# One transformer block pair on one core: norms read from PSUM, Tanh for Sigmoid and Exp, the second residual moved to VectorE, and a last output block in one PSUM region

## The reference, cut to what matters

```python
y = conv_gated_mlp(rms_norm(h, ln_ffn_pre), w_up, conv_w, conv_b, w_down)
h = h + rms_norm(y, ln_ffn_post)
h = h + (p @ w_pe) * sigmoid(h @ w_pg)            # end of the first block
...                                               # second block: projections u @ w_in
conv, forgetting and memory heads: head output * silu(gate)
h = h + concat(heads) @ w_out
return rmsnorm(h, final_g)                        # final_g is a vector of 2048
```

## Time and profile before

| | us |
|---|---|
| median of 3 runs | 1853.12 (1852.43 to 1854.91) |
| profiled execution, its own time | 1853.38 |
| its span, first to last instruction | 1851.6 |
| TensorE busy in the span | 1800.9 |
| VectorE, ScalarE, GpSimd busy | 1282.6, 960.8, 653.2 |
| mean granted TensorE clock | 0.992 of full |

### The profile page before, as it was taken

One profiled execution on the slowest core, in us unless ns is written; L12 is line 12 of the kernel. 1 busy time (PEld: TensorE's weight loads), 2 busy tenths in 40 slices (PEclk: granted clock), 3 DMA queues, 4 the chain that ended last, 5 costly groups with the idle time before them and its releaser, 6 DMA issues.

```text
span 1851.6 us, 29943 instructions
## 1 busy us (share of the span) xinstructions
PE 1800.9 (97%) x10306; PEld 1569.7 (85%) x10306; DVE 1282.6 (69%) x1584; ACT 960.8 (52%) x1276; POOL 653.2 (35%) x639
## 2 busy tenths in 40 slices
PE   9999999999989999999999999999899999999996
PEld 7888888888878888888888888888788888878885
DVE  6676666665578777777777544446787778888754
ACT  5564555445456555555555433335555666764532
POOL 3723444444743333211111322223452255450033
PEclk9999999999999999999999999999899999999998
DMA  8434444445554555555555455555455444443452
GB/s 316 146 132 159 160 161 164 172 160 205 187 206 179 193 187 181 184 192 190 181 183 195 163 187 187 187 187 191 145 193 195 144 175 159 159 159 137 161 188 105
DMA packets 50284, 326.56 MB, mean 176 GB/s; under 512 B 5696, under 2 KB 6336, under 8 KB 17600
## 3 DMA queue, kind: packets, MB, share of 16 engines
q1 hardware_dynamic: 49664, 323.86, 49.4%
q10 hardware_dynamic: 576, 2.11, 0.3%
HBM read 323.85 MB, written 2.10 MB: 176 GB/s over the span
## 4 chain that ended last, share of the span: by engine, by line
PE 83%; DVE 7%; issue 4%; ACT 3%; DMA 1%; SPq 1%; POOL 0%; DVEq 0%; ACTq 0%; POOLq 0%
PE ps L1759 52%; PE ps L1760 27%; DVE wlo L926 2%; PE ps_lev L1834 2%; ACT whi L438 1%; DMA stage<-in_w_a 1%; DVE fge L949 1%; DVE fs L1477 1%; PE ps_t L1788 0%; ACT usq L814 0%; DVE fge L1481 0%; DVE tmp L932 0%; DVE y L1219 0%; ACT small L445 0%; PE ps_t L2065 0%
## 5 line engine op out<-in xcount | busy, mean ns | idle before, releaser
L1759 PE MATMUL ps<-act_a,whi 128*128 128x512 f32 x3072 | 1092.3, 397 | 10.7 <-DVE tmp L932 8.4
L926 DVE TENSOR_TENSOR wlo<-stage,whi 128x2048 fp32r<-128x2048 f32 (+1 forms) x316 | 701.5, 2221 | 248.8 <-ACT whi L438 244.9
L1760 PE MATMUL ps<-act_a,wlo 128*128 128x256 f32 x3072 | 869.3, 283 | 0.0
L1759 PEld LDWEIGHTS ps<-act_a,whi 128*128 128x128 f32 x3072 | 578.5, 188 | 144.9 <-DVE tmp L932 7.7
L438 ACT ACTIVATE whi<-stage 128x2048 fp32r<-128x2048 f32 (+1 forms) x316 | 568.9, 1801 | 122.4 <-DMA stage<-in_w_down 105.5
L1760 PEld LDWEIGHTS ps<-act_a,wlo 128*128 128x128 f32 x3072 | 579.0, 188 | 0.3
L1759 PE MATMUL ps<-big,whi 128*128 128x512 f32 x1600 | 566.0, 396 | 9.1 <-DVE big L1333 7.3
L1760 PE MATMUL ps<-big,wlo 128*128 128x256 f32 x1600 | 453.4, 283 | 0.0
L1759 PEld LDWEIGHTS ps<-big,whi 128*128 128x128 f32 x1600 | 301.5, 188 | 80.1 <-DVE big L1333 5.6
L445 ACT ACTIVATE small<-ps 128x256 f32<-128x256 f32 x248 | 94.8, 382 | 520.4 <-PE ps L1760 520.3
L1760 PEld LDWEIGHTS ps<-big,wlo 128*128 128x128 f32 x1600 | 301.9, 189 | 0.1
(11 more groups left out here) (338 smaller groups left out, 1400.9 us busy)
## 6 DMA issues: line engine op xcount, KB each, us to landing
stage<-in_w_a SPq DMA_DIRECT2D x166, 1024.0 KB, 4.8
stage<-in_w_b SPq DMA_DIRECT2D x87, 1024.0 KB, 4.8
stage<-in_w_down SPq DMA_DIRECT2D x64, 704.0 KB, 4.0
stage<-in_w_a SPq DMA_DIRECT2D x8, 256.0 KB, 9.7
mem_raw<-in_memT SPq DMA_DIRECT2D x1, 2048.0 KB, 9.2
mem_again<-in_memT SPq DMA_DIRECT2D x1, 2048.0 KB, 9.1
out<-o_out SPq DMA_DIRECT2D x4, 512.0 KB, 2.7
x_in<-in_xT ACTq DMA_DIRECT2D x3, 512.0 KB, 8.8
```

Source lines behind the costliest of these rows:

```text
L926: dve.tensor_tensor(wlo[:, slot, part], stage[:, slot, part], whi[:, slot, part].bitcast(F32), ALU.subtract).then_inc(w_lo, 1)
L1759: pe.matmul(dst, whi[:, slot, c * P:(c + 1) * P], act, start=start, stop=False)
L1760: return pe.matmul(dst[:, T:2 * T], wlo[:, slot, c * P:(c + 1) * P], act[:, 0:T], start=False, stop=stop)
```

## The change

It is one diff with these parts. They are numbered as the prediction takes them.

1. Norms: `mean_square` is gone for all norms but "uc". ACT's Ln reads the sum from PSUM with scale 1/2048 and a bias column `eps`. `ln_ahead()` loads the Ln table earlier (start, before `G_OUT`, after the first residual, last down block, before conv, before `G_OUT2`). POOL's squares of `h4` wait on "h3_norm".
2. Gates: Sigmoid and the Exp of the gates become Tanh. The gate is made with (tanh + 1) by one `scalar_tensor_tensor` on DVE, with factors 0.5 and 0.25 in neighbouring instructions. `logistic` (add one, reciprocal) is gone.
3. The "y" stage: the last tile of `y` is squared by ACT; all of the residual is on DVE, quarter after quarter; the 16 outputs of `w_pe` lie in pairs in seven banks and ACT copies two at once; the first two blocks of `w_pg` are run together, quarter by quarter.
4. `fox_turned` of the last head stands in the middle of the second memory block; `memory_turned` and `memory_out` of the last memory head move one block later.
5. The last block of `G_OUT2` goes to one region of 256 columns: identity by `h`'s last tile, then three matmuls of 256 columns for a cell. ACT squares it from PSUM. DVE alone scales the output, in five pieces; there are five output DMAs.

```diff
+        eps = sb("eps", [P, 1])
+        y_sq = over("y_sq", a_at, 23 * KB, [P, T])
+        out_parts = (slice(0, 4), slice(4, 8), slice(8, 12), slice(12, 14), slice(14, 16))
+        pair_banks = [*wide_banks, ps_sc[:, :], ps_t[:, :], bank_b[:, :], ps[:, 0, :], ps[:, 1, :]]
@@ sync
-            for c in range(QUARTERS):
-                sp.wait_ge(*(s("o_ready"), c + 1) if c < QUARTERS - 1 else (s("o_last"), 1))
-                sp.dma_start(out[:, quarter(c), :], o_out[:, quarter(c), :]).then_inc(s("out_done"), 16)
+            for n, part in enumerate(out_parts):
+                sp.wait_ge(s("o_ready"), n + 1)
+                sp.dma_start(out[:, part, :], o_out[:, part, :]).then_inc(s("out_done"), 16)
@@ scalar
-            def norm(t, name):
-                inverse_root(t, event(name + "_ms"), event(name + "_norm")[0])
+            def ln_ahead():
+                act.preload_act_table(ACT.Ln)
+
+            def norm(t, name, sums):
+                act.wait_ge(*event(name + "_summed"))
+                link(act.activation(t, sums, ACT.Ln, scale=1.0 / D, bias=eps[:, 0:1]))
+                act.activation(t, t, ACT.Exp, scale=-0.5).then_inc(event(name + "_norm")[0], 1)
@@
-            def sigmoid(e, x, lin, done, i):
+            def tanh(e, x, lin, done, i, scale=1.0):
                 wait(act, lin, i + 1)
-                act.activation(e[:, :], x[:, :], ACT.Sigmoid).then_inc(s(done), 1)
+                act.activation(e[:, :], x[:, :], ACT.Tanh, scale=scale).then_inc(s(done), 1)
@@ last down block
-                        act.activation(dummy[:, 1:2], ones[:, 0:1], ACT.Ln)
+                        ln_ahead()
+                        act.wait_ge(out_free, U_DOWN + KT + 2)
+                        act.wait_ge(*step("y_acc", KT - 1))
+                        act.activation(y_sq[:, :], y[:, KT - 1, :], ACT.Square).then_inc(step("y_acc", 0)[0], 1)
@@
-            keep(range(3))
-            norm(rstd[:, :], "y")
-            keep(range(3, 7))
+            norm(rstd[:, :], "y", ps_a)
             hi(G_PE, 0, 0, 3)
-            keep(range(7, 11))
+            keep(range(4))
             split_h2(0)
-            keep(range(11, 13))
+            keep(range(4, 7))
             split_h2(1)
-            keep(range(13, 16))
+            keep(range(7, 8))
             split_h2(2)
             split_h2(3)
@@
-            for j in range(4):
+            for j in range(3):
                 evac(U_OUT2 + 12 + j, j % 2, G_OUT2 - U_OUT2)
...
-            act.wait_ge(s("h4_ready"), KT)
-            act.activation(sq4[:, 1, :], h4[:, KT - 1, :], ACT.Square).then_inc(event("h4_last_sq")[0], 1)
-            norm(rstd[:, :], "h4")
+            act.wait_ge(w_used, N_BLOCKS)
+            act.activation(sq4[:, 1, :], ps[:, 1, 0:T], ACT.Square).then_inc(event("h4_last_sq")[0], 1)
+            norm(rstd[:, :], "h4", ps_a)
@@ vector
+            def twice_gated(e, x, tanh_done, n):
+                dve.wait_ge(s(tanh_done), n)
+                link(dve.scalar_tensor_tensor(out=e, in0=e, scalar=1.0, in1=x, op0=ALU.add, op1=ALU.mult))
@@
-            dve.wait_ge(*event("y_summed"))
-            mean_square(ps_a, rstd[:, :], "y_ms")
             lo(G_PE, 0, 0, 2)
             dve.wait_ge(*step("y_gain", KT))
             dve.wait_ge(*event("y_norm"))
-            normed(y, 0, "y_scaled")
-            normed(y, 1, "y_scaled")
-            add_first(y, "y_scaled", "h2_first")
-            normed(y, 2, "y_scaled")
+            scaled_by_norm(y, 0)
+            residual(y, 0, "h2_made")
+            lo(G_PE, 0, 0, 3)
+            scaled_by_norm(y, 1)
             split_h2(0)
-            lo(G_PE, 0, 0, 3)
+            residual(y, 1, "h2_made")
+            scaled_by_norm(y, 2)
             split_h2(1)
+            residual(y, 2, "h2_made")
+            scaled_by_norm(y, 3)
             split_h2(2)
+            residual(y, 3, "h2_made")
             split_h2(3)
             lo(G_PE, 0, 0, 4)
@@ fox_head, memory heads
-                logistic(fge[:, :], "fg_exp", i + 1)
-                link(dve.tensor_tensor(fge[:, :], fge[:, :], fgx[:, :], ALU.mult))
+                twice_gated(fge[:, :], fgx[:, :], "fg_tanh", i + 1)
@@
-            for c in range(QUARTERS - 1):
-                dve.tensor_tensor(o_out[:, quarter(c), :], h4[:, quarter(c), :], by_norm, ALU.mult).then_inc(s("o_ready"), 1)
+            for part in out_parts[:-1]:
+                by = rstd[:, :].unsqueeze(1).to_broadcast([P, part.stop - part.start, T])
+                dve.tensor_tensor(o_out[:, part, :], h4[:, part, :], by, ALU.mult).then_inc(s("o_ready"), 1)
+            link(dve.tensor_tensor(o_out[:, KT - 2, :], h4[:, KT - 2, :], rstd[:, :], ALU.mult))
+            dve.scalar_tensor_tensor(out=o_out[:, KT - 1, :], in0=ps[:, 1, 0:T], scalar=column("final_g", KT - 1),
+                                     in1=rstd[:, :], op0=ALU.mult, op1=ALU.mult).then_inc(s("o_ready"), 1)
@@ tensor
-            column_sums(ps_a, [acc[:, :]], lambda n: step("y_acc", KT), "y_summed")
+            column_sums(ps_a, [acc[:, :], y_sq[:, :]], lambda n: step("y_acc", KT - 1 + n), "y_summed")
@@
-            for j in range(4):
-                whole(G_PG, 0, 0, j, U_PG + j, j % 2, xs_h,
-                      ready=None if j else lambda c: pe.wait_ge(s("xs_h"), c * QUARTERS // KT + 1))
+            for c in range(QUARTERS):
+                for j in range(2):
+                    if c == 0:
+                        pe.wait_ge(s("pe_kept"), len(pair_banks) - 1 + j)
+                        await_block(G_PG, 0, 0, j, U_PG + j)
+                    ins = cells((G_PG + j) % NS, j, xs_h, range(KT)[quarter(c)], opens=c == 0, closes=c == QUARTERS - 1,
+                                ready=None if j else lambda c: pe.wait_ge(s("xs_h"), c * QUARTERS // KT + 1))
+                    if c == QUARTERS - 1:
+                        ins.then_inc(w_used, 1)
+            for j in range(2, 4):
+                whole(G_PG, 0, 0, j, U_PG + j, j % 2, xs_h)
@@
-                memory_turned(n - 1) if n else fox_turned(HEADS - 1)
-                whole(G_MEM, 0, 0, 2 * n + 1, u + 1, 1, act_a)
+                if n:
+                    memory_turned(n - 1)
+                    whole(G_MEM, 0, 0, 2 * n + 1, u + 1, 1, act_a)
+                else:
+                    await_block(G_MEM, 0, 0, 1, u + 1)
+                    cells((G_MEM + 1) % NS, 1, act_a, range(KT // 2), closes=False)
+                    fox_turned(HEADS - 1)
+                    cells((G_MEM + 1) % NS, 1, act_a, range(KT // 2, KT), opens=False).then_inc(w_used, 1)
@@
-                if k == 0:
+                if k == 1:
                     memory_turned(MEM_HEADS - 1)
-                if k == 1:
+                if k == 2:
                     memory_out(MEM_HEADS - 1)
@@
+            await_block(G_OUT2, 3, 4, 3, U_OUT2 + 15)
+            slot = (G_OUT2 + 3) % NS
+            last_out = ps[:, 1, 0:T]
+            pe.matmul(last_out, ident[:, :], h[:, KT - 1, :], start=True, stop=False)
+            for c in order:
+                cell = slice(c * P, (c + 1) * P)
+                pe.matmul(last_out, whi[:, slot, cell], xs_y[:, c, 0:T], start=False, stop=False)
+                pe.matmul(last_out, whi[:, slot, cell], xs_y[:, c, T:2 * T], start=False, stop=False)
+                ins = pe.matmul(last_out, wlo[:, slot, cell], xs_y[:, c, 0:T], start=False, stop=c == order[-1])
+            ins.then_inc(w_used, 1)
```

More of the change, by code:

```diff
@@ L627, in _ @@
                     hi(G_OUT + 4, i, 4, j + 3)
[L628 removed]
+            norm(rstd[:, :], "mixed", ps_a)
             def split_h1(c):
[L631 removed]
+                act.wait_ge(*step("h1_made", c + 1))
                 for k in range(KT)[quarter(c)]:
@@ L780, in _ @@
                 act.wait_ge(s("cv_lin"), n + 1)
-                act.activation(ce[:, :], cx[:, 1, :], ACT.Sigmoid).then_inc(s("cv_sig"), 1)
+                act.activation(ce[:, :], cx[:, 1, :], ACT.Tanh, scale=0.5).then_inc(s("cv_sig"), 1)
                 if n == 0:
@@ L841, in fox_head @@
                 wait(act, "fg_lin", i + 1)
-                act.activation(fge[:, :], fgx[:, :], ACT.Exp, scale=-1.0).then_inc(s("fg_exp"), 1)
+                act.activation(fge[:, :], fgx[:, :], ACT.Tanh, scale=0.5).then_inc(s("fg_tanh"), 1)
                 wait(act, "fv_turned", i + 1)
@@ L878, in _ @@
                 act.wait_ge(s("mg_lin"), n + 1)
-                act.activation(fge[:, :], fgx[:, :], ACT.Exp, scale=-1.0).then_inc(s("mg_exp"), 1)
+                act.activation(fge[:, :], fgx[:, :], ACT.Tanh, scale=0.5).then_inc(s("mg_tanh"), 1)
                 act.wait_ge(s("mv_turned"), n + 1)
@@ L884, in _ @@
             act.wait_ge(s("cl_ready"), GROUPS)
-            act.activation(usq[:, :, :], uc[:, :, :], ACT.Sigmoid).then_inc(event("cl_sig")[0], 1)
+            act.activation(usq[:, :, :], uc[:, :, :], ACT.Tanh, scale=0.5).then_inc(event("cl_sig")[0], 1)
             for k in range(GROUPS):
@@ L1056, in query_made @@
             def query_made(i):
```

(16 more changed lines are left out.)

193 lines of the change are left out of this document (90 added, 103 removed).

## The result

The changed kernel takes 1807.66 us (median of 4 runs, 1806.3 to 1807.98) against 1853.72 for the kernel before (1852.43 to 1854.91): ratio 0.975, 95% interval 0.9733 to 0.9767. The forecast was 1825.5, range 1820.5 to 1832.5. The direction was right, and the gain of 46 was 1.6 times what was forecast. The profiled execution has a span of 1806.2, 45.4 less than before.

The account below looks back on a forecast made before the run. TensorE, busy 97% of the span, was taken as the bound, so only its idle and lower-clock time could be won. Terms a to h summed to 27.6 us, 1853.38 to 1825.8, or 1825.5 against the median; range 1820.5 to 1832.5.

Parts of the forecast that it names:

- term a: First norm: ScalarE reads the sum from PSUM itself, so TensorE's gap of 1.2 goes: -1.2 us.
- b: Norm at "mixed": L952 and two handoffs leave the chain, so it starts 1.5 earlier: -1.5 us (-0.7 to -2.5).
- d: "y" stage: earlier norm, GpSimd out, `w_pg` blocks run by quarters: -9.8 us (-4.8 to -10.5).
- e: Forgetting heads: without the logistic VectorE comes earlier and six `add` waits of 1.05 go: -6.3 us.
- f: `fox_turned` of the last head: wait of 2.4 and the lower clock behind it go: -3.9 us (-2.4 to -4.1).
- g: `memory_out` of the last memory head a block later: its wait goes, -1.5 us (-0.5 if half comes again).
- h: Kernel's end: earlier sum and Ln, VectorE alone scaling in pieces, smaller last DMA: -2.8 us (-1.8 to -3.8).
- the clock near 100: Clock fall near 100 us, behind the 3.8 wait for the first head's scores: forecast to stay, 0 gained.
- c: Norm at "h1": one L952 of 0.42 and its handoffs go: -0.6 us (-0.3 to -0.9).
- 1 (the clock falls in the `w_pg` quarters): Rival: the clock drops in the new `w_pg` quarters all the same, 4.8 us more: 1830.3; chance 0.14.

Follow-up runs that it names:

- (0, 32): Changed kernel laid out with activations at distance 0 from `wlo` and 32 from `whi` (remainders by 128 bytes): 1810.77 us, one run.
- (32, 0): Changed kernel laid out with activations at distance 32 from `wlo` and 0 from `whi` (remainders by 128 bytes): 1825.99 us, one run.
- (64, 32): Changed kernel with `eps` in `dummy`, `whi` 32 and activations 64 bytes further; distances 64 from `wlo`, 32 from `whi` by 128: 1822.35 us.
- (96, 96): Changed kernel with `act_a` and `big` another 64 bytes further; distance 96 from both `wlo` and `whi` by 128: 1825.82 us, one run.
- the run with three waits of 1.8 to 1.9 between the quarters: Changed kernel with the first two `w_pg` blocks one after the other, not interleaved by quarters: 1811.31 us, ratio 0.9766.
- the run with two reciprocals: Changed kernel with two more VectorE reciprocals behind each forgetting head's gate product, on a tile not read again: 1825.52 us, ratio 0.9839.
- (32, 32): The changed kernel's own layout, activations at distance 32 from both `wlo` and `whi` by 128 bytes, against (0, 0) before: 1807.66 us.

## Why the prediction was wrong, point by point

**The step that failed** stands ahead of term a: "Stretches that no term names I leave as they are." TensorE is busy 97% of the time, so its rate in those stretches is the largest number in the kernel, and I took 5.62 a block as fixed. The change touches it: `eps` is a tile of its own, and it moves what TensorE reads by 32 bytes against what it loads. With the column elsewhere the time is 1824.11, inside the range and 1.4 from the forecast; the mechanisms that I named were right, and the missing term, 16.5 us by experiment, put the time outside. That the rate depends on the place of the activations against the weights is shown by the runs without any other edit (12.3 us; and none where all moves together). Why it does isn't: that the load of `whi` meets the read of the activations agrees with the shorter `wlo` matmul at (0, 32) and with the mirror (32, 0), but not with (64, 32) to (96, 96), where both matmuls change, nor with two rates at one distance.

**Terms.** By the changed kernel's trace a, b, d, e, f, g and h came out within 0.3 of the forecast. The run with `eps` in `dummy` needs no allowance for shorter blocks and is the better test. There b, c, d, f and g are within 0.3, h is 0.5 more, a 0.7 more and e 1.5 more, while the clock near 100, which was to stay as it was, cost 1.4. These errors partly cancel; that the sum came so near is in part luck.

**e was too small** because a wait costs more than its row says. Before, at a head's wait:
```profile
1588.24 0.49 PE L1788 MATMUL ps_t<-ident,fs 128*128 128x128 f32 x3
1589.77 0.50 PE L1759 MATMUL ps<-act_a,whi 128*128 128x512 f32 x1 [1.04 <-DVE tmp L932]
```
With `eps` in `dummy`, where the wait is gone:
```profile
1571.86 0.49 PE L1787 MATMUL ps_t<-ident,fs 128*128 128x128 f32 x3
1572.11 0.48 PE L1758 MATMUL ps<-act_a,whi 128*128 128x512 f32 x1
```
From the transposes' start to the block's is 1.53 with the wait and 0.25 without. That is 1.28 for a wait of 1.04, and the six heads gained 1.30 each: the 1.04 is counted from the end of the last matmul's row, and without a wait the next one starts inside that row.

**d.** VectorE's products after the change are 1.22 and 1.23, with GpSimd away from `y`, as taken:
```profile
1276.15 1.22 DVE L1233 TENSOR_TENSOR y<-y,rstd 128x1024 f32<-128x1024 f32 x1
1277.40 1.23 DVE L1342 TENSOR_TENSOR big<-x_in,big 128x1024 fp32r<-128x1024 f32 x1
1278.54 1.22 DVE L1236 TENSOR_TENSOR x_in<-x_in,y 128x1024 f32<-128x1024 f32 x1
```
That is 3.5 a quarter, with four waits of 0.4 to 1.2 and the clock at 1.00; before, L1219's pair took 4.59.

**c came out, and the shorter block took it back.** I took L952 out of the chain to "h1" and let 0.6 of 0.9 go. The wait before the `add` fell from 0.9 to 0.4, but in the changed kernel TensorE waits 1.0 for GpSimd's last sum. GpSimd's row and VectorE's beside it, after, and then before:
```profile
548.76 2.87 POOL L1614 TENSOR_TENSOR acc<-mixed 128x256 f32<-128x256 f32 x1
...
548.75 5.02 DVE L942 TENSOR_TENSOR wlo<-stage,whi 128x2048 fp32r<-128x2048 f32 x2 [1.38 <-ACT whi L440]
```
```profile
555.09 0.74 POOL L1598 TENSOR_TENSOR acc<-mixed 128x256 f32<-128x256 f32 x1
...
555.15 2.83 DVE L926 TENSOR_TENSOR wlo<-stage,whi 128x2048 fp32r<-128x2048 f32 x1 [1.38 <-ACT whi L438]
```
Before, GpSimd began 0.06 ahead and took 0.74, and VectorE's `wlo` 2.83. Now VectorE begins 0.01 ahead and GpSimd takes 2.87. The same two rows stand in all eighteen traces. In eight GpSimd begins 0.02 to 0.13 ahead; it takes 0.73 to 0.74, VectorE 2.76 to 2.87, and TensorE doesn't wait. In ten VectorE begins ahead or within 0.002 of it; it takes 2.29, GpSimd 2.82 to 2.87, and TensorE waits 1.0 to 1.1. So whoever starts second is held, and a few hundredths of a us decide who. The parts of the change don't bring this. With `eps` in `dummy` all of them are there, GpSimd takes 0.74, no wait for `acc` stands, and c is 0.6 as forecast; in the kernel before with nothing but 32 bytes of padding GpSimd takes 2.87:
```profile
552.96 0.74 POOL L1615 TENSOR_TENSOR acc<-mixed 128x256 f32<-128x256 f32 x1
```
```profile
552.25 2.87 POOL L1599 TENSOR_TENSOR acc<-mixed 128x256 f32<-128x256 f32 x1
```
In all ten a block took 5.547 or less in the stage ahead (430 to 508); of the eight this holds for one, the kernel before with weights 32 and activations 64 further. So the shorter block made the collision likely and not certain.

**The rivals.** 1 (the clock falls in the `w_pg` quarters) did not come, even in the run with three waits of 1.8 to 1.9 between the quarters; but behind waits of that length in the heads the clock did fall twice, so this was no safe bet.
## What to carry to other kernels

Where one engine is busy all the time, its rate in the quiet stretches is a term of the sum like any other: count its instructions in one window that never waits, before and after, ahead of looking at any wait. A change that allocates anything moves what lies behind it; look at what moved against what, and try two or three paddings in a kernel that is bound by matmuls. Look at more than one stretch of each trace: a layout can have one rate in one stage and another in the next. A wait is worth some more than its row says. And gains add up unevenly: a faster TensorE alone gave 12.3, with VectorE's chains shortened first it gave 16.5.

## What the runs showed of the hardware that I had not expected

- With weights 128 x 128 and fp32r activations, a cell of two matmuls takes 0.343 to 0.353 us (a block of 5.493 to 5.653) at the full clock, with the same instructions and other distances of activations and weights in SBUF, in steps of 32 bytes. 128 bytes more, from (32, 32), gave the same block. At four of the eight distances tried, one trace has two rates.
- The length of a wait doesn't tell whether the clock falls behind it. It stayed at 1.00 with TensorE busy 5.74 of 12 us in waits of up to 1.9; in the run with two reciprocals it fell behind waits of 1.94 and 1.92 and not behind others of 1.94 and 1.92. It fell behind one of 3.2, and where one of 5.1 stood.
- A wait of 1.04 in its row cost TensorE 1.30, one of 0.10 cost 0.37.
- GpSimd's addition over 128 x 256 took 0.74 when it began at least 0.02 ahead of VectorE's `wlo` and 2.82 to 2.87 when it began with it or behind it, in eighteen traces; VectorE's products of 1024 columns beside GpSimd's took as long as 2.3 each, and 1.22 without.
